# Parameter columns multiplied on TensorE at the start of six stages of a hybrid SSD and Hyena layer

## The chip, the cores and the metric

The kernel runs on one core of one Trainium2 chip. Its time is the device time of one execution in microseconds (us), as the median of several. The profile is a record of one execution, which the hardware profiler took. In what follows, PE is TensorE, PEld its weight loads, DVE VectorE, ACT ScalarE, POOL GpSimd, and SP the engine that issues most of the DMAs. A "record" is one entry of the trace: a 32-bit multiplication shows there as two matmuls with a weight load each.

## What is computed

One layer of a diffusion backbone with 2048 latent tokens of width 1024 and 256 context tokens. Two token mixers, a bidirectional Mamba-2 scan and an order-2 Hyena convolution, read the same normalized input through one projection; their outputs are gated, projected, merged and added to the input.

```python
h = rmsnorm(x, norm_w) * (1.0 + scale[:, None]) + shift[:, None]
...
cols = in_projection(h, w_in, ALL_IN_NAMES)
...
filt = hyena_filters(seqlen, w1, b1, w2, b2, w3, b3, freq, w_out)
h_bias = h_bias.astype(jnp.float32)
z = v
for o, gate in enumerate((x1, x2)):
    z = gate * (bidir_long_conv(z, filt[:, 0, o], filt[:, 1, o]) + h_bias[o] * z)
...
scores = jnp.einsum("bcqgn,bcsgn->bcqsg", cmat, bmat)
y_diag = jnp.einsum("bcqsg,bcqsgr,bcsgrp->bcqgrp", scores, decay, xdt)
y_off = jnp.einsum("bcqgn,bcgrpn,bcqgr->bcqgrp", cmat, start_states, jnp.exp(a_cs))
...
merged = (jax.nn.sigmoid(cols["g_m"]) * (ym @ w_branch_m)
          + jax.nn.sigmoid(cols["g_h"]) * (yh @ w_branch_h))
return merged @ w_out
```

## The kernel before

The kernel is a chain of stages, each a function with one instruction block per engine. A stage frees its semaphores at its end and all engines meet at a barrier (`Phase.release`, lines 68 and 67 in the trace); then the next stage's blocks begin. Nothing of a stage, not even a load, starts before that barrier, apart from a few loads of the first stages. Within a stage every engine's order is written out by hand, and semaphores tie the engines together. Data goes from one stage to the next through scratch tensors in HBM.

After the modulation, the normalization and the large input projection (until about 1630 us) come the six stages that matter here:

- **Taps** (`phase_taps_and_steps`, from 1636.6 us). PE multiplies the filters' hidden layer with the output weights (lines 1172 and 1174), eight matmuls of 512 columns into four banks, with the hidden layer split in a high part (line 1105, ACT) and a low part (line 1229, DVE). DVE multiplies each result with a decay window (line 1250) that ACT makes, and SP stores it as `kern_s`.
- **Spectra** (`phase_filter_spectra`, from 1785.8 us). The filters' Fourier transforms. SP loads `kern_s` in chunks into a ring of four buffers `spec_xin`; the load for chunk n waits until PE has used chunk n-4 (`s_a`). For each chunk PE runs `first` twice, each time four fp32 multiplications of 128x128 by 128 columns (line 1310), eight records. ACT and DVE copy the results out, and `second` (line 1323) multiplies them with a table. In the first block of 8 chunks there is only `first`; from the second block on, `first` of the block and `second` of the block before alternate.
- **Convolutions** (`phase_long_convs`, from 2029.4 us). Eight convolutions. PE's `first` (line 1527) is 64x64 matmuls on quarters of the array, `forward` is line 1567; DVE multiplies with the spectra (`product`, line 1696), for which SP loads six slots ahead, then the gate's inputs, then the next block's x, then further slots, in one queue.
- **States** (`phase_states`, from 2518.2 us). The scan's states, chunk by chunk: ACT and DVE weigh the inputs (lines 1833, 1858), PE multiplies (line 1807), DVE adds to the state (line 1877). The chunks' loads are all issued by SP, each into a buffer of its own.
- **Scan outputs** (`phase_ssd_outputs`, from 2634.6 us). PE makes scores (line 1978), then segment sums (line 1990) from masks that POOL and ACT spread (lines 1947, 2054), and the outputs from these.
- **Merge** (`phase_merge_output`, from 2917.0 us). 96 tiles of 24 matmuls each (lines 2304 to 2306: high and low parts of both operands). For the first tile DVE and ACT make high and low parts one `k` after another. After tile 0 PE forms two sums of squares (line 2314) from additions of POOL (line 2281), then goes on to tile 1.

In each of these stages PE's block begins with a wait for the stage's first loads or for what is made from them. `keep["par"]` is a small array of per-channel parameters, 128 partitions by 64 columns (`NPAR`) in fp32, that is loaded in the first stage and stays in SBUF.

Of the kernel before, what the change touches and what calls it, by code (L numbers as in the profile page):

```python
# [51 lines left out]

def banks(ph, n):
    return [ph.ps(f"bank{i}", [P, 512]) for i in range(n)]


class Phase:
# [951 lines left out]
def phase_taps_and_steps(nc, t, keep, tables, hid_s, kern_s, dt_c, dt_s, step_s):  # L1009
# [8 lines left out]
    with ExitStack() as ctx:  # L1018
# [106 lines left out]

        @block.tensor
        def _(pe):
            def reuse(k):
                if k >= 2:
                    name, i = slots[k - 2]  # L1130
                    if name == "taps":
                        pe.wait_ge(s_res, i + 1)
                    elif name == "turned":
                        pe.wait_ge(s_v, 2)
                    else:
                        pe.wait_ge(s_e, 3 * i + 3)
# [121 lines left out]
                    nc.vector.memset(res[:, o, SEQ:SEQ + 1], 0.0).then_inc(s_fix, 1)  # L1258


def phase_filter_spectra(nc, tables, kern_s, spec_s):

    NI = 2 * NBK
    GP = CB // 2
# [1 line left out]
    with ExitStack() as ctx:  # L1266
# [5 lines left out]
        bank = banks(ph, 8)  # L1272
# [25 lines left out]

        @block.tensor
        def _(pe):  # L1300
            def first(i, q):
                n = 16 * i + q
                if q % 2 == 0:
                    pe.wait_ge(s_ld[n // 2 % 4], loaded(n // 2))
                if n >= 4:
                    pe.wait_ge(s_ea, n - 3)
                    pe.wait_ge(s_ev, n - 3)
                for s in range(4):
                    g = 8 * (q % 2) + 2 * s
                    mm = pe.matmul(bank[n % 4][:, s * P:(s + 1) * P],  # L1310
                                   xin[:, n // 2 % 4, g:g + 2, :].rearrange("p g n -> p (g n)"), fk[:], start=True,
                                   stop=True)
                mm.then_inc(s_a, 1)
# [52 lines left out]
                    take(nc.vector.tensor_copy, i, q, 1, 1).then_inc(s_ev, 1)  # L1366


def phase_long_convs(nc, tables, u_s, z2_s, spec_s):

    NQ, NR, SLOT = 16, 8, 6
    NH, PS = NPL // 2, 4
    with ExitStack() as ctx:
# [134 lines left out]

        @block.tensor
        def _(pe):  # L1510
            def first(j, q):
                n, (blk, o) = NQ * j + q, convs[j]
                if o == 0 and q % 4 == 0:
# [216 lines left out]
def phase_states(nc, t, keep, tok_s, st_s, step_s, ssd):  # L1730
# [7 lines left out]
    with ExitStack() as ctx:  # L1738
# [49 lines left out]

        @block.tensor
        def _(pe):  # L1790
            def gates(s):
                for i in range(KT * KT * (s - G0) // GS, KT * KT * (s - G0 + 1) // GS):
                    m, k = i // KT, i % KT
                    if m % 4 == 0 and k == 0:
                        pe.wait_ge(s_aw[m // 4], 16)
                    mm = pe.matmul(gate[:, 2 * m:2 * m + 2], aw[:, m // 4, k, m % 4 * P:(m % 4 + 1) * P],
                                   keep["silu"][:, k, :], start=(k == 0), stop=(k == KT - 1))
                    if i == KT * KT - 1:
                        mm.then_inc(s_gate, 1)
# [85 lines left out]
            dve.wait_ge(s_gout, 1)  # L1885


def phase_ssd_outputs(nc, t, xbc_s, tok_s, st_s, z_s, g_s, ssd):

    with ExitStack() as ctx:  # L1890
        ph = Phase(nc, "y", ctx)
# [77 lines left out]

        @block.tensor  # L1970
        def _(pe):
            def scores(c):
                q = c % 2
                pe.wait_ge(s_bc[q], 16 * (c // 2) + 16)
# [177 lines left out]
def phase_merge_output(nc, t, keep, ym_s, z2_s, hg_s, gates_s, out):  # L2152
# [6 lines left out]
    with ExitStack() as ctx:  # L2159
# [132 lines left out]

        @block.tensor
        def _(pe):
            def tile(s, b, br, j):
                pe.wait_ge(s_wlo, s + 1)
                if s >= 4:
# [342 lines left out]
def program(nc, t, out):  # L2640
# [19 lines left out]
    with ExitStack() as ctx:  # L2660
# [18 lines left out]
        with ExitStack() as tctx:  # L2679
            tables = hyena_tables(Phase(nc, "tab", tctx))  # L2680
            phase_taps_and_steps(nc, t, keep, tables, hid_s, kern_s, dt_c, dt_s, step_s)
            phase_filter_spectra(nc, tables, kern_s, spec_s)
            phase_long_convs(nc, tables, u_s, z2_s, spec_s)
        with ExitStack() as sctx:
            ssd = ssd_buffers(Phase(nc, "ssd", sctx))
            phase_states(nc, t, keep, tok_s, st_s, step_s, ssd)
            phase_ssd_outputs(nc, t, xbc_s, tok_s, st_s, z_s, ym_s, ssd)
        phase_merge_output(nc, t, keep, ym_s, z2_s, hg_s, g_s, out)


# [28 lines left out]
```

## Time and profile before

| | us |
|---|---|
| Median of 3 executions | 3513.61 |
| Lowest and highest | 3512.41, 3515.05 |
| The profiled execution | 3513.2 |
| Its span, first to last instruction | 3511.1 |
| PE busy in it | 3228.8 (92%) |
| Mean granted clock of PE | 0.963 |

The granted clock is the share of full speed at which the throttle lets PE run; it has two levels here, 0.50 (1.2 GHz) and 1.00 (2.4 GHz). In a row of the timeline the bracket says how long the engine stood idle before the instruction and what released it. A wait for several semaphores is put down to the one that came last.

### The profile page before, as it was taken

To read this page: it belongs to the slowest core of one execution; us is meant where nothing else is said; L and a number is where in the kernel's file an instruction comes from. 1 tells how busy PE (TensorE), PEld (TensorE's weight loads), DVE (VectorE), ACT (ScalarE), POOL (GpSimd) and SP (SyncE) were. 2 spreads that over 40 slices of the span, in tenths; PEclk is the share of its full clock that TensorE was granted. 3 is DMA by queue.
4 is the path that set the end of the run, shared out by engine and by line. 5 is a ranking of instruction groups with operands and counts; after the bars stand their busy time and mean duration, and the time that the engine had idled before them with its cause. 6 is when DMAs were issued, how large, how long until landed. Compare 5 with 4: busy or idle time off the path is not lost. (4 is left out here: it accounts for less than half of the span.)

```text
span 3511.1 us, 55790 instructions
## 1 busy us (share of the span) xinstructions
PE 3228.8 (92%) x21878; PEld 2602.8 (74%) x21878; DVE 2080.1 (59%) x2495; ACT 1452.9 (41%) x2709; POOL 1948.4 (55%) x1324
## 2 busy tenths in 40 slices
PE   7899999999699999996679979999778997999998
PEld 3677888888588888885469956767566886788886
DVE  6697886223896884222754435555566775667662
ACT  4423222333433223333347745545447763333332
POOL 0486999777787998773100024343467763444542
PEclk9999999999799999998889989999989998999998
DMA  8444333332243323334899974664675665666562
GB/s 298 150 148 149 114 108 116 112 114 102 102 150 126 114 102 120 114 109 128 335 290 298 271 170 121 160 163 117 201 311 174 198 188 192 200 204 198 190 189 98
DMA packets 530472, 592.22 MB, mean 169 GB/s; under 512 B 287403, under 2 KB 408131, under 8 KB 527171
## 3 DMA queue, kind: packets, MB, share of 16 engines
q1 hardware_dynamic: 438957, 430.82, 40.7%
q10 hardware_dynamic: 91256, 157.83, 12.1%
q8 instruction: 176, 2.88, 0.4%
q14 instruction: 83, 0.68, 0.1%
HBM read 383.76 MB, written 204.80 MB: 168 GB/s over the span
## 5 line engine op out<-in xcount | busy, mean ns | idle before, releaser
L759 PE MATMUL pl_bank<-hl_hi,pl_a_hi 128*128 128x512 f32 x2056 | 813.6, 396 | 41.5 <-DVE hl_lo L391 27.8
L761 PE MATMUL pl_bank<-hl_hi,pl_a_lo 128*128 128x512 f32 x2056 | 804.9, 392 | 0.0
L760 PE MATMUL pl_bank<-hl_lo,pl_a_hi 128*128 128x512 f32 x2056 | 804.2, 391 | 0.0
L704 POOL TENSOR_TENSOR pl_a_lo<-hl_early_x,pl_a_hi 128x512 fp32r<-128x512 f32 x288 | 434.4, 1520 | 115.7 <-ACT pl_a_hi L808 115.6
L759 PEld LDWEIGHTS pl_bank<-hl_hi,pl_a_hi 128*128 128x128 f32 x2056 | 388.2, 189 | 129.3 <-DVE hl_lo L391 28.0
L761 PEld LDWEIGHTS pl_bank<-hl_hi,pl_a_lo 128*128 128x128 f32 x2056 | 388.4, 189 | 82.5
L760 PEld LDWEIGHTS pl_bank<-hl_lo,pl_a_hi 128*128 128x128 f32 x2056 | 389.0, 189 | 78.0
L808 ACT ACTIVATE pl_a_hi<-hl_early_x 128x512 fp32r<-128x512 f32 x288 | 181.8, 633 | 540.3 <-PE pl_bank L761 444.6
L2276 POOL TENSOR_TENSOR mo_w_lo<-mo_w,mo_w_hi 128x1024 fp32r<-128x1024 f32 x96 | 238.1, 2482 | 277.1 <-ACT mo_w_hi L2347 277.1
L704 POOL TENSOR_TENSOR pl_a_lo<-hl_w,pl_a_hi 128x512 fp32r<-128x512 f32 x220 | 312.3, 1433 | 114.6 <-ACT pl_a_hi L808 114.5
L2304 PE MATMUL mo_bank<-mo_hi,mo_w_hi 128*128 128x512 f32 x768 | 305.8, 398 | 20.6 <-POOL mo_w_lo L2276 17.2
L958 DVE SCALAR_TENSOR_TENSOR pl_res<-hl_early_w,pl_taps,pl_res 128x1023 f32<-128x1023 f32 (+1 forms) x160 | 312.3, 1952 | 3.0
L2306 PE MATMUL mo_bank<-mo_hi,mo_w_lo 128*128 128x512 f32 x768 | 300.7, 392 | 0.0
L2305 PE MATMUL mo_bank<-mo_lo,mo_w_hi 128*128 128x512 f32 x768 | 300.5, 391 | 0.0
L1506 POOL TENSOR_TENSOR conv_both<-conv_prod 128x256 f32<-128x256 f32 x128 | 93.6, 732 | 282.8 <-DVE conv_prod L1691 207.2
L808 ACT ACTIVATE pl_a_hi<-hl_w 128x512 fp32r<-128x512 f32 x220 | 138.0, 629 | 258.8 <-PE pl_bank L761 252.0
L699 POOL TENSOR_TENSOR hl_early_x<-hl_w 128x512 f32<-128x512 f32 x144 | 214.7, 1491 | 12.2 <-POOL pl_a_lo L704 12.2
L1696 DVE TENSOR_TENSOR conv_prod<-conv_front,conv_spec 128x1024 f32<-128x1024 f32 x120 | 141.9, 1219 | 90.5 <-PE conv_front L1567 67.2
L2304 PEld LDWEIGHTS mo_bank<-mo_hi,mo_w_hi 128*128 128x128 f32 x768 | 144.8, 189 | 56.6 <-issue 18.2
L1665 ACT COPY conv_v<-conv_inv 128x512 f32<-128x512 f32 x128 | 126.2, 1066 | 141.3 <-PE conv_inv L1583 141.3
L1336 DVE COPY spec_y<-spec_bank 64x256 f32<-64x256 f32 x256 | 109.5, 428 | 124.0 <-PE spec_bank L1310 121.9
L2305 PEld LDWEIGHTS mo_bank<-mo_lo,mo_w_hi 128*128 128x128 f32 x768 | 145.1, 189 | 30.9 <-issue 1.9
(237 smaller groups left out, 6026.4 us busy)
## 6 DMA issues: line engine op xcount, KB each, us to landing
hl_w<-in_w_rec SPq DMA_DIRECT2D x146, 512.0 KB, 3.6
mo_w<-in_w_br SPq DMA_DIRECT2D x96, 512.0 KB, 3.7
kern_s<-taps_res SPq DMA_DIRECT2D x16, 2048.0 KB, 7.0
spec_s<-spec_res ACTq DMA_DIRECT2D x128, 256.0 KB, 3.7
conv_spec<-spec_s SPq DMA_DIRECT2D x240, 128.0 KB, 2.9
g_s<-pl_res ACTq DMA_DIRECT2D x32, 512.0 KB, 2.6
spec_xin<-kern_s SPq DMA_DIRECT2D x32, 512.0 KB, 5.9
spec_xin<-kern_s SPq DMA_DIRECT2D x128, 128.0 KB, 3.8
```

Source lines behind the costliest of these rows:

```text
L699: nc.gpsimd.tensor_tensor(sums[:, i], x, y, op).then_inc(s_sum, 1)
L704: nc.gpsimd.tensor_tensor(a_lo[:, at % NS, :], src, a_hi[:, at % NS, :].bitcast(F32), ALU.subtract).then_inc(s_lo, 1)
L759: pe.matmul(out, a_hi[:, q, m], op_hi[:, b, k, :], start=begin, stop=False)
L760: pe.matmul(out, a_hi[:, q, m], op_lo[:, b, k, :], start=False, stop=False)
L761: return pe.matmul(out, a_lo[:, q, m], op_hi[:, b, k, :], start=False, stop=end)
L808: nc.scalar.activation(a_hi[:, n % NS, :], src, ACT.Copy).then_inc(s_hi, 1)
L958: nc.vector.scalar_tensor_tensor(out=dst, in0=src[:, i:i + width], scalar=taps[i], in1=dst, op0=ALU.mult, op1=ALU.add).then_inc(s_conv, 1)
L1696: nc.vector.tensor_tensor(prod[:, n % PS], u[:, None].to_broadcast([P, 2, 2, CB]), spec[:, m % SLOT, :, None].to_broadcast([P, 2, 2, CB]), ...
L2276: nc.gpsimd.tensor_tensor(w_lo[:, s % 3, :], w[:, s % 3, :], w_hi[:, s % 3, :].bitcast(F32), ALU.subtract).then_inc(s_wlo, 1)
L2304: pe.matmul(bank[s % 4][:], w_hi[:, q, m], hi[:, slot, k, :], start=(k == 0), stop=False)
L2305: pe.matmul(bank[s % 4][:], w_hi[:, q, m], lo[:, slot, k, :], start=False, stop=False)
L2306: mm = pe.matmul(bank[s % 4][:], w_lo[:, q, m], hi[:, slot, k, :], start=False, stop=(k == KT - 1))
```

## The change

A helper issues n times the same multiplication: 128 partitions, 64 stationary columns and 64 moving columns, both of them `keep["par"]`, into a 64x64 corner of a PSUM bank. Nothing reads the corner; the stage's real work overwrites it or leaves it alone. The multiplications wait for nothing and signal nothing. PE's block of six stages begins with such a call, ahead of everything else; `keep` is passed to the three functions that did not have it. The counts are 80 (taps), 75 (spectra), 30 (convolutions), 48 (states), 30 (scan outputs) and 82 (merge).

```diff
+def keep_busy(pe, out, src, n):
+
+    for _ in range(n):
+        pe.matmul(out, src, src, start=True, stop=True)
...
+            keep_busy(pe, ps[1][0:NPAR, 0, 0:NPAR], keep["par"][:, 0:NPAR], 80)
...
-def phase_filter_spectra(nc, tables, kern_s, spec_s):
+def phase_filter_spectra(nc, keep, tables, kern_s, spec_s):
...
         @block.tensor
         def _(pe):
+            keep_busy(pe, bank[7][0:NPAR, 0:NPAR], keep["par"][:, 0:NPAR], 75)
+
             def first(i, q):
...
+            keep_busy(pe, front[1][0:NPAR, 1, 0:NPAR], keep["par"][:, 0:NPAR], 30)
...
+            keep_busy(pe, gate[0:NPAR, 64:64 + NPAR], keep["par"][:, 0:NPAR], 48)
...
+            keep_busy(pe, p_seg[0][0:NPAR, 0:NPAR], keep["par"][:, 0:NPAR], 30)
...
+            keep_busy(pe, bank[3][0:NPAR, 0:NPAR], keep["par"][:, 0:NPAR], 82)
```

Line numbers in the changed kernel are 6 to 18 higher. In PE's order, the start of the spectra stage before, where the two branches are the stage's boundary, `spec_bank` the stage's eight banks and `spec_xin` the loaded chunks:

```order
L1174 MATMUL taps_ps<-taps_hid_lo,taps_ws 128x512
L1018 UNCONDITIONAL_BRANCH
L1299 UNCONDITIONAL_BRANCH
L1310 MATMUL spec_bank<-tab_fk,spec_xin 128x128 x68
L1323 MATMUL spec_bank<-spec_y,tab_wf 128x256 x2
L1310 MATMUL spec_bank<-tab_fk,spec_xin 128x128 x4
```

And in the changed kernel:

```order
L1182 MATMUL taps_ps<-taps_hid_lo,taps_ws 128x512
L1024 UNCONDITIONAL_BRANCH
L1307 UNCONDITIONAL_BRANCH
L60 MATMUL spec_bank<-keep_par 64x64 x75
L1320 MATMUL spec_bank<-tab_fk,spec_xin 128x128 x68
L1333 MATMUL spec_bank<-spec_y,tab_wf 128x256 x2
```

The 75 stand ahead of the first chunk's matmuls, and nothing else has moved. PE's start of the scan output stage before, where `y_p_sc` are the scores and `y_p_seg` the segment sums:

```order
L1738 UNCONDITIONAL_BRANCH
L1970 UNCONDITIONAL_BRANCH
L1978 MATMUL y_p_sc<-y_bc 128x128 x4
L1990 MATMUL y_p_seg<-y_spread,ssd_after 128x512 x16
L1978 MATMUL y_p_sc<-y_bc 128x128 x4
```

And in the changed kernel:

```order
L1750 UNCONDITIONAL_BRANCH
L1984 UNCONDITIONAL_BRANCH
L60 MATMUL y_p_seg<-keep_par 64x64 x30
L1994 MATMUL y_p_sc<-y_bc 128x128 x4
L2006 MATMUL y_p_seg<-y_spread,ssd_after 128x512 x16
L1994 MATMUL y_p_sc<-y_bc 128x128 x4
```

The 30 stand ahead of the first scores; between these and the segment sums nothing was put.

## Rows read from the trace of the kernel before

**Rows 1.** The page: the whole execution's span.
```profile
span 3511.1 us, 55790 instructions
```
**Rows 2.** Stretches: length, busy by PE, PEld, DVE, ACT, POOL, granted clock, DMA share, GB/s.
```profile
1785.80:1790.06 4.26, 0.00 (x1) 0.00 (x1) 0.00 (x0) 0.00 (x0) 0.00 (x0) 0.50 0.83 172
1790.06:1793.80 3.74, 3.74 (x17) 3.74 (x18) 0.85 (x2) 0.80 (x2) 0.00 (x0) 0.50 1.37 223
1793.80:1797.40 3.60, 3.60 (x33) 3.45 (x31) 3.35 (x8) 3.23 (x8) 0.00 (x0) 1.00 1.38 217
2033.60:2046.40 12.80, 10.42 (x355) 10.09 (x356) 4.42 (x10) 4.42 (x10) 0.00 (x0) 0.50 0.89 175
2644.20:2647.10 2.90, 2.89 (x7) 2.33 (x8) 0.12 (x1) 0.81 (x3) 2.90 (x2) 0.50 1.02 407
2928.00:2933.80 5.80, 5.58 (x12) 3.56 (x12) 5.47 (x7) 2.84 (x4) 2.42 (x1) 0.50 1.05 392
```
**Rows 3.** Timeline, spectra stage, SP and PE: start, us, engine, instruction, [idle <-releaser].
```profile
1785.79 0.37 SPq L1291 DMA_DIRECT2D spec_xin<-kern_s  x1
1790.06 3.57 PE L1310 MATMUL spec_bank<-tab_fk,spec_xin 128*128 128x128 f32 x15 [21.32 <-DMA spec_xin<-kern_s]
1793.87 0.77 SPq L1291 DMA_DIRECT2D spec_xin<-kern_s  x1
...
1799.84 2.05 PE L1310 MATMUL spec_bank<-tab_fk,spec_xin 128*128 128x128 f32 x16 [0.36 <-DMA spec_xin<-kern_s]
...
1809.47 1.16 PE L1310 MATMUL spec_bank<-tab_fk,spec_xin 128*128 128x128 f32 x8 [0.36 <-DMA spec_xin<-kern_s]
```
**Rows 4.** PE's instruction groups, 1812 to 2009 us: busy, mean ns, idle.
```profile
L1310 PE MATMUL spec_bank<-tab_fk,spec_xin 128*128 128x128 f32 x884 | 116.6, 275 | 0.0
```
**Rows 5.** Weight loads of 128 and 64 columns, ns min/median/max.
```profile
L1310 PEld LDWEIGHTS spec_bank<-tab_fk,spec_xin x1024: 186/192/333, 1790.1 to 2006.6; 128*128 128x128 f32 x171
L1567 PEld LDWEIGHTS conv_front<-conv_y,tab_wf x1024: 132/137/230, 2052.0 to 2487.8; 128*64 128x64 f32 x171
```
**Rows 6.** Timeline, taps stage: PE's second set, VectorE's first products.
```profile
1659.86 0.80 PE L1172 MATMUL taps_ps<-taps_hid_hi,taps_ws 128*128 128x512 f32 x1 [6.37 <-DVE taps_hid_lo L1229]
1662.18 4.49 DVE L1250 TENSOR_TENSOR taps_res<-taps_ps,taps_window 128x2048 f32<-128x2048 f32 x2 [2.38 <-ACT taps_window L1110]
```
**Rows 7.** Timeline, convolution stage: SP's loads, VectorE's wait.
```profile
2065.90 4.30 SPq L1446 DMA_DIRECT2D conv_spec<-spec_s  x4
2072.75 3.49 DVE L1696 TENSOR_TENSOR conv_prod<-conv_front,conv_spec 128x1024 f32<-128x1024 f32 x3 [8.60 <-DMA conv_spec<-spec_s]
```
**Rows 8.** Timeline, state stage: SP's first load, VectorE.
```profile
2518.15 0.33 SPq L1769 DMA_DIRECT2D ssd_tail<-step_s  x1
2529.91 1.22 DVE L1877 TENSOR_TENSOR st_state<-st_faded,st_s 128x1024 f32<-128x1024 f32 x1 [0.51 <-PE st_s L1807]
2533.11 0.82 DVE L1858 TENSOR_TENSOR st_wx<-st_xb,st_tail 128x640 f32<-128x640 f32 x1 [1.98 <-DMA st_xb<-tok_s]
```
**Rows 9.** Timeline, scan output stage, PE's first matmuls.
```profile
2638.93 2.08 PE L1978 MATMUL y_p_sc<-y_bc 128*128 128x128 f32 x8 [5.93 <-DMA y_bc<-xbc_s]
2644.21 3.43 PE L1990 MATMUL y_p_seg<-y_spread,ssd_after 128*128 128x512 f32 x8 [3.20 <-ACT y_spread L2054]
```
**Rows 10.** Timeline, merge stage: SP's first load, PE, POOL's additions.
```profile
2916.95 0.36 SPq L2215 DMA_DIRECT2D mo_yT<-z_s  x1
2928.04 0.76 PE L2304 MATMUL mo_bank<-mo_hi,mo_w_hi 128*128 128x512 f32 x1 [16.07 <-POOL mo_w_lo L2276]
...
2938.88 5.01 POOL L2281 TENSOR_TENSOR mo_ms<-mo_ms,mo_odd 128x512 f32<-128x512 f32 x4 [4.74 <-ACT mo_odd L2367]
2940.48 2.10 PE L2314 MATMUL mo_ssq<-mo_ms,mo_ones 128*128 128x512 f32 x4
2942.02 0.80 PE L2304 MATMUL mo_bank<-mo_hi,mo_w_hi 128*128 128x512 f32 x1
```
**Rows 11.** Waits, 2915 to 2990 us: total us, times, longest.
```profile
PEld mo_ssq L2314 <- POOL mo_ms L2281: 0.9, 2, 0.7
```

More of the change, by code:

```diff
@@ L1366, in _, with phase_long_convs @@
                     take(nc.vector.tensor_copy, i, q, 1, 1).then_inc(s_ev, 1)
-def phase_long_convs(nc, tables, u_s, z2_s, spec_s):
+def phase_long_convs(nc, keep, tables, u_s, z2_s, spec_s):
     NQ, NR, SLOT = 16, 8, 6
@@ L1885, in _, with phase_ssd_outputs @@
             dve.wait_ge(s_gout, 1)
-def phase_ssd_outputs(nc, t, xbc_s, tok_s, st_s, z_s, g_s, ssd):
+def phase_ssd_outputs(nc, t, keep, xbc_s, tok_s, st_s, z_s, g_s, ssd):
     with ExitStack() as ctx:
@@ L2681, in program @@
             phase_taps_and_steps(nc, t, keep, tables, hid_s, kern_s, dt_c, dt_s, step_s)
-            phase_filter_spectra(nc, tables, kern_s, spec_s)
-            phase_long_convs(nc, tables, u_s, z2_s, spec_s)
+            phase_filter_spectra(nc, keep, tables, kern_s, spec_s)
+            phase_long_convs(nc, keep, tables, u_s, z2_s, spec_s)
         with ExitStack() as sctx:
@@ L2686, in program @@
             phase_states(nc, t, keep, tok_s, st_s, step_s, ssd)
-            phase_ssd_outputs(nc, t, xbc_s, tok_s, st_s, z_s, ym_s, ssd)
+            phase_ssd_outputs(nc, t, keep, xbc_s, tok_s, st_s, z_s, ym_s, ssd)
         phase_merge_output(nc, t, keep, ym_s, z2_s, hg_s, g_s, out)
```

## The prediction

> **What bounds the kernel now.** I start from the span, 3511.1 us [rows 1], and ask of each of the six stages what releases it at its start and what it runs at after that. I read the granted clock in short stretches first, since the change can only work through it. PE does start on the lower level of its clock (0.50, 1.2 GHz): in the spectra stage it does nothing from SP's first load at 1785.79 to its first matmul at 1790.06, and its clock stands at 0.50 until 1793.8, then at 1.00 (2.4 GHz) [rows 2, 3]. The scan output stage (2644.2 to 2647.1) and the merge stage (2928.0 to 2933.8) show the same [rows 2]. So the clock rises 2.9 to 5.8 us after PE begins to work, 3.7 in the spectra stage. The second question is whether those cold matmuls are late for anybody. That is read from the timelines, from who waits last.
>
> In the spectra stage it is the loads: PE's chunks of 16 records begin at 1799.84 and on to 1809.47, each after some 0.36 us of waiting for spec_xin [rows 3], with the DMA share at 1.37 to 1.38 [rows 2]. Five chunk starts lie in 9.63 us, 2.4 us each. After that PE sets the pace: from 1812 to 2009 us it has no idle time before the 884 records of line 1310 [rows 4]. What the stage loses before 1810 is therefore lost at its end.
>
> **What a parameter matmul costs.** It isn't in the trace. A 64x64 fp32 multiplication of 128 rows should be two records, as line 1310's are (884 in the stretch where the code has half as many), each with a weight load. The nearest row is line 1310, with 128 columns: 17 records in 3.74 us, 0.220 us each, at 0.50, and 33 in 3.60 us, 0.109 us each, at 1.00 [rows 2]. Half the columns halves both the stream and the load of the weights (median 192 ns for 128 columns against 137 for 64: 55 ns for 64 columns) [rows 5]. I take 0.110 us cold and 0.055 warm per record. The upper bound is the whole price of line 1310. The lower one is line 1527, the small 64x64 matmuls of the convolution stage: 355 records in 10.42 us, 0.029 us each, at 0.50 [rows 2]. Line 1527 works on quarters of the array, several at a time, while the new ones all use the same half, so I stay with the half price.
>
> **Spectra stage, 75 of them, 150 records.** PE can start them when the stage begins, about 1785.8, with the clock at 0.50. If it rises after 4.4 us (the middle of 2.9 and 5.8), 40 records are done by then, and 110 more take 6.0 us: PE is free at 1796.3. With 2.9 and 5.8 us it is 1795.5 and 1797.0. The first chunk has been there since 1790.06, so PE comes 5 to 7 us late. It is then warm, but that isn't enough, since the ring of four buffers stops the loads: SP's fifth load waits until PE has used up the first chunk. Now it is issued at 1793.87, about 0.3 us after 1790.06 + 16 x 0.22 = 1793.6, and its data starts the chunk at 1799.84 [rows 3]. Afterwards the first chunk ends at 1796.3 + 16 x 0.109 = 1798.0 and the load is issued at 1798.3. By then the queue has run dry (the fourth chunk's data is in at about 1797.4, one pace of 2.4 us before 1799.84), and a load into an idle queue takes 1790.06 - 1785.79 = 4.27 us [rows 3]: 1802.6. That is 2.7 us behind 1799.84 (2.0 to 3.4 with the other two rises). From there the loads go at their old pace of 2.4 us and PE, with 1.75 us of work in each, can't make them come sooner. The warm start itself is worth nothing here. **+2.7 us**, kept to the end of the stage.
>
> **Taps stage, 80.** Nothing. They lie in PE's wait for its first weights; after its first eight matmuls PE waits another 6.37 us for VectorE's low halves, starting again at 1659.86, and VectorE's first products at 1662.18 are released by ScalarE's window [rows 6]. PE's eight next matmuls end before the second product.
>
> **Convolution stage, 30.** PE's first 512 records get shorter, by at most half of the 10.42 us at 0.50 [rows 2], 5.2 us. But VectorE then stands 8.60 us, until 2072.75, for a spectrum load that SP issues at 2065.90 behind its other loads, in an order and at a pace that PE has no hand in [rows 7]. Anything from 5.2 us early to 8 us late vanishes in it. Zero.
>
> **State stage, 48.** 96 records are 4.4 + 56 x 0.055 = 7.5 us from 2518.15: 2525.7. Sixteen records of 256 columns at twice 0.109 end at 2529.2, no later than VectorE's second state at 2529.91. It next waits for a load until 2533.11 anyway [rows 8]. Zero.
>
> **Scan output stage, 30.** Some 3.3 to 6.6 us (60 records at either price), against PE's 5.93 us of idle time before 2638.93; the scores from there on get 1 us shorter. Then PE waits for ScalarE's spreads until 2644.21 [rows 9]. It is at 0.50 there now [rows 2]. If it stayed at 1.00, the first segment's four matmuls would be ready some 0.85 us sooner (half of the 3.43 us for eight, for half of them), and everything behind them. But the wait before them stays, 3.20 us and more, as the scores end sooner, and an idle PE loses the clock: in the taps stage PE, idle for 6.37 us after its first eight matmuls, takes 0.80 us for the next one [rows 6], as long as the merge stage's first (0.76 us) at 0.50 [rows 10]. I take zero and keep 0.85 as the other end. The Trainium skill (TensorE: Matmul & The Clock Gate, "HAM oscillation — how this bites in real kernels") says the same against this insertion: a burst shorter than the wait behind it has to begin cold again; by that rule the sum is +2.7 us, and without it +1.9.
>
> **Merge stage, 82.** 164 records from 2916.95 take 4.4 + 124 x 0.055 = 11.2 us: 2928.2, on time for 2928.04 [rows 10]. The first tile is at 0.50 for 5.58 us [rows 2], so up to 2.8 us could be won. It is fed by VectorE, one pair of halves at a time. Behind it PE needs POOL's additions: the first of four begins at 2938.88, each takes 5.01 / 4 = 1.25 us, so the second is ready at 2941.4. PE does wait for them (0.9 us in 2 waits), and the next tile follows at 2942.02 [rows 10, 11]. An earlier end of the first tile meets that wait. Zero.
>
> The sum is +2.7 us. The profiled execution took 3513.2 us with its 3511.1 us span, 0.4 us under the median 3513.61, so I add to the median: **3516.3 us**.
>
> **Rivals.** (a) The insertions are cheap and hidden everywhere. At 0.029 us a record the 75 take 4.4 us, the length of the spectra stage's wait, and nothing moves: 3513.6. Line 1527's price speaks for it, the halves of rows 5 against it. Beside the rows: the Trainium skill (TensorE: Matmul & The Clock Gate, "Back-to-back issue gap") gives some 60 cycles, about 25 ns, for up to 64 columns; by that price too the change would be free. (b) Slower: the clock doesn't rise on these narrow matmuls. In the convolution stage it stayed at 0.50 through 12.8 us of 64-column work, PE busy for 10.42 of them [rows 2]. Then the spectra stage's 150 records end at 1802.3, the first chunk takes 3.5 us cold, and the fifth load lands at 1802.3 + 3.5 + 0.3 + 4.27 = 1810.4: +10.5 us. In the merge stage 164 x 0.110 is 18.0 us, PE starts at 2935.0, and the tile's 24 matmuls, twelve in 5.6 us as now and twelve in half of that, end at 2943.4; with 1.5 us for the sums (2940.48 to 2942.02) that is 2.9 us late: 3527.0. The full price of line 1310 would give about as much. It decides from 0.083 us per warm record, twice that cold: 4.4 us cold and 10.3 warm for the 150, PE free at 1800.5, and a loss of 7.0 us in the spectra stage alone. Against it: there is no gap in these matmuls, and in all stages the clock rose within 5.8 us of dense work. (c) Faster: the cold stretches are on the path after all. Half of 3.74, 10.42, 2.89 and 5.58 us is 11.3 us; with the 2.7 lost, 3505.0. It needs VectorE and POOL to wait for PE where the rows show loads and additions.
>
> **How the numbers follow.** The forecast, 3516.3, gets 0.62: its own range is 3515.5 to 3517.2. (a) gets 0.15, (b) 0.15, (c) 0.05; 0.03 is for other shifts, such as PE's instruction fetches falling elsewhere. A measurement of this kernel can tell about 0.2%, 7.0 us. Forecast and (a) lie within it. (b) lies above, but a mild form of it doesn't. (c) is just beyond. So faster 0.05, same 0.80, slower 0.15. The range goes from 3511.5, which takes in (a) with the 1.2 us by which the runs of before fall under their median, to 3521.0, where the spectra stage costs 7.4 us by a dearer record.
>
> **What would show it.** In the timeline the 150 records run from 1785.8 to 1796.3, PE's first real matmul there starts at about 1796, five to seven us later than its data, and SP's fifth load is issued at about 1798. The stage's end, and every later stage, lies 2.7 us later. PE's clock is at 1.00 when it starts on spectra and on the merge tile. VectorE's wait of 8.6 us in the convolution stage stays, about as long; the scan's first segments are still at 0.50; the second merge tile starts as long after the stage's begin as before, 25.1 us. I would be wrong if PE's first real matmul there stayed at its load's landing (a), if the clock were 0.50 until after it (b), or if the stretch from the stage's start to the second tile shrank (c).

## The result, and the profile of the changed kernel

| | before | changed |
|---|---|---|
| Median of 20 executions each, us | 3513.05 | 3519.61 |
| Lowest and highest, us | 3509.3, 3518.46 | 3515.37, 3524.35 |
| Span of the profiled execution, us | 3511.1 | 3517.4 |
| Mean granted clock of PE | 0.963 | 0.971 |

The ratio is 1.0017 with a 95% interval of 1.0011 to 1.0023. On 3513 us that is 6.0 us more, 3.9 to 8.1. The clock did rise, and the kernel got slower. The time lies within the predicted range and within the 0.2% called no change, but 3.3 us above the forecast of 3516.3 and outside the forecast's own range, and where 2.7 us were forecast to be lost, 6.0 were.

The page's first line and its line on the queue of TensorE's instruction fetches (packets, MB, share). The queue had 176 packets in the kernel before:

```profile
span 3517.4 us, 57170 instructions
...
q8 instruction: 181, 2.97, 0.4%
```

Stretches of the changed kernel, with the columns of [rows 2]:

```profile
1781.50:1786.50 5.00, 4.98 (x47) 5.00 (x48) 0.00 (x0) 0.00 (x0) 0.00 (x0) 0.50 0.91 183
1786.50:1792.60 6.10, 6.10 (x106) 6.08 (x104) 0.00 (x0) 0.00 (x0) 0.00 (x0) 1.00 1.20 195
1792.60:1796.30 3.70, 3.70 (x35) 3.65 (x33) 2.35 (x6) 2.24 (x6) 0.00 (x0) 1.00 0.11 26
2641.50:2644.40 2.90, 0.81 (x2) 0.74 (x3) 1.17 (x2) 1.94 (x7) 2.90 (x1) 0.50 1.12 361
2932.10:2937.90 5.80, 3.82 (x12) 1.94 (x12) 5.64 (x7) 2.73 (x4) 2.41 (x1) 1.00 1.05 396
```

A parameter record costs 4.98 / 47 = 0.106 us at 0.50 and 6.10 / 106 = 0.058 us at 1.00. PE now begins the spectra and the merge stage at 1.00, where [rows 2] had 0.50. The third row is the important one: while PE is at full clock on its first real chunks, the DMA share is down to 0.11, where it was 1.38 for the first chunks at full clock before. The scan output stage's first segments are still at 0.50.

The start of the spectra stage, PE's timeline and one load of SP (the fifth of the stage), to be held against [rows 3]:

```profile
1781.52 11.20 PE L60 MATMUL spec_bank<-keep_par 128*64 128x64 f32 x150 [15.17 <-PEq L74]
1792.65 10.98 PE L1320 MATMUL spec_bank<-tab_fk,spec_xin 128*128 128x128 f32 x96
1803.95 2.05 PE L1320 MATMUL spec_bank<-tab_fk,spec_xin 128*128 128x128 f32 x16 [0.31 <-DMA spec_xin<-kern_s]
1806.39 2.05 PE L1320 MATMUL spec_bank<-tab_fk,spec_xin 128*128 128x128 f32 x16 [0.40 <-DMA spec_xin<-kern_s]
1809.64 1.16 PE L1320 MATMUL spec_bank<-tab_fk,spec_xin 128*128 128x128 f32 x8 [1.19 <-DMA spec_xin<-kern_s]
```

```profile
1794.73 0.36 SPq L1299 DMA_DIRECT2D spec_xin<-kern_s  x1
```

SP's first load is at 1781.48, so PE's first real matmul comes 11.2 us into the stage, and the fifth load is issued 13.25 us into it. Before, these were 4.3 and 8.1 us [rows 3]. Six chunks (96 records) then run without a wait. From the seventh on, PE waits for loads again. The ninth chunk, with which the stage's PE-bound part begins, starts at 1809.64, 28.2 us after the stage's first load; before it was 1809.47 - 1785.79 = 23.7. So 4.5 of the 5.0 us by which the stage is longer (248.6 against 243.6) are there by the ninth chunk. PE's matmuls of `first` from 1815 to 2009 us have no idle time before them, as in [rows 4]:

```profile
L1320 PE MATMUL spec_bank<-tab_fk,spec_xin 128*128 128x128 f32 x872 | 114.9, 275 | 0.0
```

The rows that answer to [rows 6, 7, 9], from the timelines of the taps, convolution and scan output stage:

```profile
1659.69 0.80 PE L1180 MATMUL taps_ps<-taps_hid_hi,taps_ws 128*128 128x512 f32 x1 [6.33 <-DVE taps_hid_lo L1237]
...
2073.07 3.48 DVE L1708 TENSOR_TENSOR conv_prod<-conv_front,conv_spec 128x1024 f32<-128x1024 f32 x3 [5.68 <-DMA conv_spec<-spec_s]
...
2643.59 3.51 PE L2006 MATMUL y_p_seg<-y_spread,ssd_after 128*128 128x512 f32 x8 [2.25 <-ACT y_spread L2070]
```

And the merge stage's first tile, for [rows 10, 11]: two rows of PE's timeline and one of the waits.

```profile
2939.28 0.50 PE L2322 MATMUL mo_bank<-mo_hi,mo_w_hi 128*128 128x512 f32 x1 [2.40 <-DVE mo_lo L2445]
...
2940.48 0.79 PE L2322 MATMUL mo_bank<-mo_hi,mo_w_hi 128*128 128x512 f32 x1 [0.24 <-DVE mo_lo L2445]
```

```profile
PEld mo_ssq L2332 <- POOL mo_ms L2297: 1.2, 2, 0.9
```

The faster matmuls wait for VectorE's low halves, and at 2940.48 a matmul takes 0.79 us again: the clock was given back within the first tile. At its end PE waits for POOL's additions, as before.

Below, the length of each stage is taken from SP's first load of the stage to that of the next one (the merge stage to the span's end). "Ninth chunk" is the start of the 129th record of the spectra stage's `first`, counted from the stage's first load. All in us, one traced execution each; the labels are those of the experiments. The merge column can be 0.1 us low.

| kernel | taps | spectra | ninth chunk | conv. | states | scan out | merge |
|---|---|---|---|---|---|---|---|
| before | 149.2 | 243.6 | 23.7 | 488.7 | 116.4 | 282.4 | 594.0 |
| e7, before once more | 148.1 | 243.6 | 23.7 | 488.6 | 115.7 | 284.0 | 595.6 |
| changed | 145.3 | 248.6 | 28.2 | 487.2 | 116.7 | 285.6 | 597.8 |
| e1, spectra's 75 alone | 147.9 | 246.4 | 26.6 | 490.6 | 115.2 | 284.0 | 598.5 |
| e2, all but spectra's | 146.5 | 244.4 | 24.5 | 485.8 | 117.4 | 282.3 | 597.6 |
| e3, spectra's, 150 | 148.5 | 255.9 | 35.9 | 488.5 | 116.2 | 285.8 | 597.8 |
| e4, changed, ring of 8 | 147.0 | 246.2 | 25.1 | 489.3 | 116.4 | 284.2 | 597.9 |
| e5, before, ring of 8 | 147.9 | 243.9 | 23.7 | 488.3 | 115.9 | 284.2 | 595.6 |
| e6, conv.'s, 90 | 147.1 | 243.8 | 23.7 | 490.1 | 115.2 | 284.0 | 597.9 |
| e8, taps', 64 | 147.9 | 243.8 | 23.7 | 488.1 | 116.0 | 284.3 | 595.9 |
| e9, taps', 90 | 147.2 | 244.7 | 24.6 | 487.5 | 115.7 | 284.3 | 598.1 |
| e10, changed, taps' 55 | 145.9 | 247.1 | 27.2 | 490.0 | 115.9 | 283.9 | 595.1 |
| e11, 30 behind the scores | 148.0 | 243.5 | 23.7 | 488.4 | 116.1 | 284.1 | 595.4 |
| e12, the same once more | 147.5 | 243.7 | 23.7 | 489.8 | 117.0 | 282.7 | 595.7 |

Two lengths move with the kernel and not with the execution: spectra, which was predicted, and merge, which was not. The other four vary by 2 to 5 us with no such pattern. In e2 and e9 the ninth chunk is 0.8 and 0.9 us late although nothing was put into their spectra stage; that is taken up further below.

### The profile page after: what moved, and what is told of

Same layout as the page of the kernel before. It is cut to its first block and busy times, and to the rows that moved or that the text cites. A ratio compares the mean times of both kernels' runs of the same rounds, so it can differ in the third digit from the quotient of the medians.

```text
span 3517.4 us, 57170 instructions
## 1 busy us (share of the span) xinstructions
PE 3271.3 (93%) x22568; PEld 2644.2 (75%) x22568; DVE 2074.3 (59%) x2495; ACT 1451.8 (41%) x2709; POOL 1947.0 (55%) x1324
## 5 line engine op out<-in xcount | busy, mean ns | idle before, releaser
L705 POOL TENSOR_TENSOR hl_early_x<-hl_w 128x512 f32<-128x512 f32 x144 | 216.0, 1500 | 12.2 <-POOL pl_a_lo L710 12.2
```

The lines of the kernel that those rows point to most:

```text
L705: nc.gpsimd.tensor_tensor(sums[:, i], x, y, op).then_inc(s_sum, 1)
```

## Experiments on the spectra stage

The theory was the prediction's: PE late by a few us, carried to the stage's end by the ring of four buffers. Rivals: the loss is made elsewhere, or the insertions cost by themselves.

**e1 and e2: which stage loses.** e1 keeps only the 75 of the spectra stage:

```diff
-            keep_busy(pe, ps[1][0:NPAR, 0, 0:NPAR], keep["par"][:, 0:NPAR], 80)
...
-            keep_busy(pe, front[1][0:NPAR, 1, 0:NPAR], keep["par"][:, 0:NPAR], 30)
...
-            keep_busy(pe, gate[0:NPAR, 64:64 + NPAR], keep["par"][:, 0:NPAR], 48)
...
-            keep_busy(pe, p_seg[0][0:NPAR, 0:NPAR], keep["par"][:, 0:NPAR], 30)
...
-            keep_busy(pe, bank[3][0:NPAR, 0:NPAR], keep["par"][:, 0:NPAR], 82)
```

and e2 removes only these 75:

```diff
-            keep_busy(pe, bank[7][0:NPAR, 0:NPAR], keep["par"][:, 0:NPAR], 75)
```

> Only the 75 multiplications of the spectra stage are kept. My theory: nearly the whole loss comes from there, because PE comes late to the first chunk and the ring of four buffers passes the delay to the loads. In the trace of the changed kernel the eighth chunk's successor starts 28.2 us after the stage's first load against 23.7 before, and the stage is 5.0 us longer. So this kernel should be 3.5 to 5.5 us slower than before, with PE's first real matmul 11.2 us after SP's first load. Rival: the loss is spread, since in the traces the scan output stage is 3.1 us longer and the merge stage 3.7 us longer too; then this kernel is only 1 to 3 us slower than before.

Measured: 3519.27 against 3513.24, ratio 1.0016 (1.0008 to 1.0025), 5.6 us.

> The five other insertions are kept (80, 30, 48, 30, 82) and the 75 of the spectra stage left out. My theory: within 1 us of before, either way, as each of the five is hidden by a wait that PE has no part in. Rival (spread loss): 3 us or more slower, with the scan output and merge stages longer by about 3 us each, as in the one trace of the changed kernel. Second rival (the gain was real but covered by the spectra stage's loss): 2 us or more faster.

Measured: 3515.35, ratio 1.0003 (0.9995 to 1.0012). So the kernel with the spectra stage's insertion alone is slower beyond its noise, and the one with the five others isn't; but the two intervals overlap, and by the medians e2 is 2.1 us slower too. That the other five are free is not shown by these times. And e1's trace leaves something over: its ninth chunk is 2.9 us late, as forecast, and its merge stage is 598.5 us, though nothing was put there.

**e3: is every further us lost?** The 75 of e1 doubled.

```diff
-            keep_busy(pe, bank[7][0:NPAR, 0:NPAR], keep["par"][:, 0:NPAR], 75)
+            keep_busy(pe, bank[7][0:NPAR, 0:NPAR], keep["par"][:, 0:NPAR], 150)
```

> Only the spectra stage's insertion, doubled from 75 to 150. Each further multiplication is two records of 0.056 us at full clock, 0.112 us, so 75 more are 8.4 us. My theory: once PE is later than the loads need, each microsecond of it is a microsecond of the kernel, so this kernel is 8.4 us slower than the one with 75, 12 to 14 us slower than before. Rival: part of a delay is caught up behind the loads later in the stage; then the second 75 cost clearly less or more than 8.4 us.

Measured: 3527.01, ratio 1.0035 (1.0023 to 1.0048). The ninth chunk comes 35.9 us into the stage, 12.2 us late. PE's timeline of e3:

```profile
1785.25 19.03 PE L60 MATMUL spec_bank<-keep_par 128*64 128x64 f32 x300 [16.76 <-PEq L74]
1804.20 10.98 PE L1319 MATMUL spec_bank<-tab_fk,spec_xin 128*128 128x128 f32 x96
1816.33 2.05 PE L1319 MATMUL spec_bank<-tab_fk,spec_xin 128*128 128x128 f32 x16 [1.14 <-DMA spec_xin<-kern_s]
```

PE's first real matmul is 8.6 us later than in e1 (19.0 against 10.4 us after the first load), the ninth chunk 9.3 us and the stage's end 9.5 us. By the medians the kernel is 7.7 us slower than e1, where 8.4 were expected. About a us is lost for a us of delay, as a chain of loads that waits for PE would give it.

**e4 and e5: is it the ring?** e4 is the changed kernel, e5 the kernel before, both with eight buffers for `spec_xin`:

```diff
-        xin = ph.sb("xin", [P, 4, 16, NA])
+        xin = ph.sb("xin", [P, 8, 16, NA])
...
-                    if n >= 4:
-                        sp.wait_ge(s_a, 2 * (n - 4) + 2)
+                    if n >= 8:
+                        sp.wait_ge(s_a, 2 * (n - 8) + 2)
```

> The changed kernel with eight buffers for spec_xin instead of four. Theory (the ring carries the loss): the fifth to eighth loads no longer wait for TensorE, so TensorE, starting about 11.2 us after the stage's entry, reaches the ninth chunk after 8 x 1.75 us, at 25.2 us, where the loads alone would allow 23.7. The spectra stage takes 245 to 245.5 us (before 243.6, changed kernel 248.6) and the kernel is about 1.7 us slower than before, a ratio of 1.0005 and 3 to 4 us less than the changed kernel. Rival (the loss comes from the late start or from the insertions themselves, whatever the ring): the stage stays at 248 to 249 us and the ratio at 1.0015 or more.

> The kernel before with eight buffers for spec_xin and no insertion: the control of the run with eight buffers. Theory: at the stage's start the loads themselves set the pace, 2.4 us a chunk, so the deeper ring gives at most 1 us: stage 243 to 244 us, ratio 0.9997 to 1.0003. Rival: loads of this stage waited for TensorE already, and the deeper ring alone is worth 3 us or more (stage under 241 us); then the run with eight buffers and insertions says less about the insertions.

PE's timeline of e4:

```profile
1782.17 10.75 PE L60 MATMUL spec_bank<-keep_par 128*64 128x64 f32 x150 [15.22 <-PEq L74]
1792.85 15.45 PE L1320 MATMUL spec_bank<-tab_fk,spec_xin 128*128 128x128 f32 x136
```

All nine first chunks (136 records) now run without one wait. The ninth starts at 25.1 us, as expected, 1.4 us late instead of 2.9 to 4.5: the ring is what carries the rest. The stage, 246.2 us, is somewhat longer than the 245 to 245.5 expected. In e5 the ninth chunk starts at 23.7 us, so the deeper ring alone gives nothing. PE's timeline of e5, whose first load is at 1783.57:

```profile
1807.25 1.16 PE L1318 MATMUL spec_bank<-tab_fk,spec_xin 128*128 128x128 f32 x8 [0.34 <-DMA spec_xin<-kern_s]
```

As times: e5 3513.70, ratio 1.0001 (0.9992 to 1.0010), as expected. e4 3518.51, ratio 1.0017 (1.0008 to 1.0026), and that was a miss: 1.0005 was expected. The ring did what it should and the kernel stayed slow, by 5.3 us by the medians, of which the spectra stage holds 2.3. The rest had to be elsewhere.

**e6: a late start where another wait covers it.** Only the convolution stage's insertion, 90 instead of 30.

```diff
-            keep_busy(pe, front[1][0:NPAR, 1, 0:NPAR], keep["par"][:, 0:NPAR], 30)
+            keep_busy(pe, front[1][0:NPAR, 1, 0:NPAR], keep["par"][:, 0:NPAR], 90)
```

> Only the convolution stage's insertion, with 90 multiplications instead of 30: TensorE's first real matmul there comes about 12.8 us after the stage's entry instead of 4.3. Theory: with the warm clock some 3 to 5 us of that are left when TensorE hands over, and VectorE's wait of 8.6 us for its spectrum load takes it up: the wait gets shorter by that, the stage stays at 486 to 490 us, ratio 1.0000. Rival (a late start of TensorE is paid in any stage): the stage and the kernel are 4 to 8 us longer.

Measured: 3516.87, ratio 1.0006 (0.9997 to 1.0015). The convolution stage took 490.1 us; in the nine traces with no insertion there it took 487.5 to 490.6. VectorE's timeline of e6 where [rows 7] had its wait of 8.60 us:

```profile
2063.45 2.35 DVE L1706 TENSOR_TENSOR conv_prod<-conv_front,conv_spec 128x1024 f32<-128x1024 f32 x2 [0.48 <-PE conv_front L1577]
2067.39 2.36 DVE L1706 TENSOR_TENSOR conv_prod<-conv_front,conv_spec 128x1024 f32<-128x1024 f32 x2 [1.59 <-PE conv_front L1577]
2071.20 2.36 DVE L1706 TENSOR_TENSOR conv_prod<-conv_front,conv_spec 128x1024 f32<-128x1024 f32 x2 [1.45 <-PE conv_front L1577]
```

VectorE's first product there comes 32.8 us after the stage's first load, against 22.7 and 23.7 in the two traces of before. The load wait has gone altogether, and the ninth product, which had waited for that load, comes at 45.1 us against 43.3 and 43.6. So 1.5 to 1.8 of the 9 to 10 us are left, which the stage's length can't show. The 3.6 us by which the kernel is slower by the medians are not clear of noise, and the trace has a longer merge stage beside them (597.9 us). A late start of PE costs only what no later wait takes up. The expected 3 to 5 us of lateness was too little; that it would be absorbed was right.

## Experiments on the merge stage

**e7: is 594 us against 598 only the execution?** The kernel before once more.

> The kernel before once more, for a second trace of it. The lengths of its stages should repeat within about 1 us where TensorE sets the pace; the merge stage was 594.0 us in the first trace and 597.6 to 598.5 us in four traces of changed kernels, two of them without an insertion there. If it is again near 594, something in the changed kernels lengthens the merge stage by 4 us; if it is near 598, that is the variation of one execution.

Merge stage 595.6 us, as in e5, the other kernel without insertions. So the six traces with insertions by then (597.6 to 598.5) differ from the three without (594.0 to 595.6). Broken down by tile, most of it is in two places, before tile 1 and at tiles 10 and 11. A third, 0.5 to 0.8 us at tile 40, is in most traces with insertions and also in e5, which has none, so it isn't the insertions'. "To tile 1" is from the stage's first load to PE's first matmul of tile 1; "fetch" is when an instruction fetch of PE starts in the stage near its loads for tiles 10 and 11. In us:

| kernel | to tile 1 | tile 10 | tile 11 | fetch |
|---|---|---|---|---|
| before | 25.1 | 6.69 | 5.60 | 87.7 |
| e7 | 25.8 | 6.66 | 5.59 | 88.0 |
| e5 | 25.5 | 6.83 | 5.61 | 88.0 |
| e1 | 25.3 | 8.01 | 7.17 | 79.3 |
| e2 | 26.2 | 7.61 | 5.59 | 78.9 |
| e3 | 25.1 | 8.34 | 7.16 | 74.7 |
| e4 | 26.7 | 7.33 | 5.57 | 73.9 |
| e6 | 25.1 | 7.70 | 7.22 | 72.2 |
| changed | 26.4 | 8.38 | 5.61 | 75.2 |

PE's instructions come in packets of 16 KB, of which 181 instead of 176 were counted above. The changed kernel has 690 more of PE's records, and 690 / 5 is 138; between two fetches of the merge stage some 125 lie. So one packet holds about 128 records, that is 64 of these multiplications. If so, whatever is inserted before moves all later fetches, unless it is a multiple of 64. The loads for tiles 10 and 11 are issued in one burst, 71 to 81 us into the stage, and in all six of these kernels with insertions, whatever stage they were in, a fetch falls into it. The Trainium skill (Runtime: NRT & Kernel Launch, "Instruction fetch mechanics") gives the same size, 16 KiB blocks of 256 instructions, and says that crossing into a new block is mostly hidden. The first part agrees: 64 multiplications of two weight loads and two matmuls each are 256 instructions. The second is what was tested, and in this burst a fetch is not hidden.

**e8, e9, e10: a whole packet or not.** e8 and e9 have only the taps stage's insertion, with 64 and with 90; e10 is the changed kernel with 55 there, 320 in all, which is five packets.

```diff
-            keep_busy(pe, ps[1][0:NPAR, 0, 0:NPAR], keep["par"][:, 0:NPAR], 80)
+            keep_busy(pe, ps[1][0:NPAR, 0, 0:NPAR], keep["par"][:, 0:NPAR], 64)
```

> Only the taps stage's insertion, with 64 multiplications, and nothing in the other five stages. In every kernel with insertions the merge stage took 597.6 to 598.5 us, in three traces without any 594.0 to 595.6, and there TensorE's instruction fetches (one 16 KB packet for about 128 of its matmul records) fall 52.5 and 88 us into the merge stage, with insertions at 72 to 79 us, in the middle of the burst of loads for tiles 10 and 11. Theory (the place of the fetches): 64 multiplications are 128 records and so one whole fetch, which leaves the later fetches where they were: fetches at 52 to 53 and 88 us again, merge stage 594 to 596 us, no fetch in the burst; spectra stage 243.6 to 244; ratio 0.9997 to 1.0003. Rival (any insertion, or more code, lengthens the merge stage): 597.5 us or more and a ratio of 1.0005 to 1.0010.

> Only the taps stage's insertion, with 90 multiplications: 26 more than one whole fetch, the same rest as in the kernel with 90 in the convolution stage. Theory (the place of the fetches): they fall about 72 us into the merge stage, in the burst of loads; that stage takes 597.5 to 598.5 us; ratio about 1.0007. Rival (the place doesn't matter): as with 64 in the same stage, within 0.5 us in the merge stage.

> The changed kernel with 55 instead of 80 multiplications in the taps stage: 320 in all, five whole fetches, where the changed kernel has 25 more than five. Theory (two causes that add): the fetches in the merge stage are back at 52 to 53 and 88 us and that stage is 2 to 3 us shorter than in the changed kernel, 594.5 to 596 us, while the spectra stage keeps its loss (247 to 248.6 us against 243.6). In all 3 to 4 us slower than before, ratio 1.0010. Rival (no second cause): merge stage 597.5 us or more and the changed kernel's ratio, 1.0017.

The DMA queues from 71 to 81 us into the merge stage (packets, MB, share), e8:

```profile
q1 hardware_dynamic: 1475, 3.28, 90.9%
q14 instruction: 1, 0.01, 0.2%
```

and e9:

```profile
q1 hardware_dynamic: 1458, 3.24, 90.1%
q8 instruction: 1, 0.02, 0.6%
q14 instruction: 1, 0.01, 0.2%
```

e9 has the fetch (q8) and e8 doesn't. What follows in e8 (first load of the stage at 2916.50), one row each of SP, ACT and PE:

```profile
2990.60 0.44 SPq L2219 DMA_DIRECT2D mo_w<-in_w_br  x1
...
2997.00 1.06 ACT L2355 ACTIVATE mo_w_hi<-mo_w 128x1024 fp32r<-128x1024 f32 x1 [5.16 <-DMA mo_w<-in_w_br]
...
3000.56 0.50 PE L2312 MATMUL mo_bank<-mo_hi,mo_w_hi 128*128 128x512 f32 x1 [1.32 <-POOL mo_w_lo L2284]
```

and in e9 (first load at 2916.21):

```profile
2990.31 1.19 SPq L2219 DMA_DIRECT2D mo_w<-in_w_br  x1
...
2997.89 1.06 ACT L2355 ACTIVATE mo_w_hi<-mo_w 128x1024 fp32r<-128x1024 f32 x1 [4.66 <-DMA mo_w<-in_w_br]
...
3001.44 0.50 PE L2312 MATMUL mo_bank<-mo_hi,mo_w_hi 128*128 128x512 f32 x1 [2.50 <-POOL mo_w_lo L2284]
```

With the fetch, which starts 74.0 us into the stage, SP's issue at 74.1 us takes 1.19 us instead of 0.44. ACT's row is released by the weights of an earlier issue, at 72.8 us (72.7 in e8): they land 1.2 us later after the stage's start (81.7 against 80.5), and PE's wait for tile 11's low halves, behind ACT and POOL, is 2.50 us instead of 1.32. So the held issue isn't what makes them late. The burst's first load, issued at 70.7 us in e9 and 70.8 in e8, lands late too, at 76.4 against 74.7 us: all that is under way lands later. In e9 there is a second loss on top. The stretch of tile 11, e8:

```profile
3000.60:3006.10 5.50, 5.50 (x24) 4.57 (x25) 2.15 (x2) 2.10 (x3) 5.50 (x3) 1.00 0.58 156
```

and e9:

```profile
3001.40:3008.50 7.10, 7.06 (x24) 5.67 (x25) 2.24 (x2) 2.10 (x3) 6.84 (x3) 0.76 0.53 168
```

After the longer wait the clock fell to 0.50 for a part of the tile, which makes it 1.6 us longer (7.17 against 5.58 from tile to tile). Together with tile 10's 1.2 us (8.10 against 6.92) that is 2.8 us, less 0.6 gained at tiles 16 and 40: the 2.2 us by which the stages differ, 598.1 against 595.9. The spectra stage adds 0.9 us, 244.7 against 243.8.

As times, of kernels that ran side by side: e8 3511.95, ratio 1.0000 (0.9991 to 1.0008), e9 3516.39, ratio 1.0009 (1.0000 to 1.0018). That is twenty-six multiplications more, in a wait that hides them, and 4.4 us by the medians, 3.1 by the means. The two intervals overlap a good deal, so the times agree with the traces' 3.1 us (2.2 and 0.9) but wouldn't show it alone. e10: 3516.99, ratio 1.0014 (1.0005 to 1.0023), merge stage 595.1, with tile 10 at 6.80 and tile 11 at 5.59, and its ninth chunk still 3.5 us late. Its time is between e8's and the changed kernel's, as two causes that add would have it, but its interval overlaps with both of theirs; it is the trace that separates them.

**e11 and e12: full clock for the first segments.** The last prediction step to test was that a burst ahead of the scores can't warm the segments behind a wait. Here the 30 stand in that wait, and nowhere else:

```diff
+            keep_busy(pe, p_seg[0][0:NPAR, 0:NPAR], keep["par"][:, 0:NPAR], 30)
```

> 30 multiplications in the scan output stage alone, put behind the first scores, in TensorE's wait of 3.2 us for the first segments, and none elsewhere. Theory: with no idle time in front of them the first segments begin at the full clock: the first four of their matmuls, 0.43 us each at 0.50, take half, and the first segment is ready about 0.85 us sooner; the stage of 282.4 to 284.2 us gets at most 1 us shorter, which one time can't show. Rival: the clock stays at 0.50 all the same, or the 30 end after the spread's landing (6 us at the lower clock against a wait of 3.2) and the segments start up to 2 us late.

PE's timeline of e11 (first load of the stage at 2631.34):

```profile
2637.88 4.49 PE L60 MATMUL y_p_seg<-keep_par 128*64 128x64 f32 x60
2642.29 2.12 PE L2001 MATMUL y_p_seg<-y_spread,ssd_after 128*128 128x512 f32 x8
2645.57 1.20 PE L2001 MATMUL y_p_seg<-y_spread,ssd_after 128*128 128x512 f32 x4 [1.15 <-DVE y_weight L2112]
```

and of e7, without them (first load at 2632.08):

```profile
2641.70 3.75 PE L1990 MATMUL y_p_seg<-y_spread,ssd_after 128*128 128x512 f32 x8 [3.60 <-ACT y_spread L2054]
2645.82 1.86 PE L1990 MATMUL y_p_seg<-y_spread,ssd_after 128*128 128x512 f32 x4 [0.36 <-DVE y_weight L2100]
```

The eight matmuls take 2.12 us instead of 3.75, and start 1.3 us later (10.95 against 9.62 us), because the 60 records ran over the spread's landing. The next segments start 14.2 us into the stage against 13.7. Nothing is gained: both halves of the expectation came true and cancel.

Its trace was also the exception in the other matter: 30 multiplications, a fetch at 72.5 us, and yet a merge stage of 595.4 us. So the same kernel was timed:

> The kernel with 30 multiplications behind the first scores once more, now timed. Its first trace is the exception to the theory of the fetches' place: a fetch 72.5 us into the merge stage, in the burst of loads, and yet a merge stage of 595.4 us. Theory 1 (a fetch in the burst costs 2 to 3 us, in most executions): this trace shows 597.5 to 598.5 us and the timed ratio is 1.0005 to 1.0010, less the 0.85 us that the warm segments may give. Theory 2 (it is not enough that the fetch falls into the burst, and this kernel escapes every time): 595 to 596 us again and a ratio of 0.9995 to 1.0003.

Measured: 3513.36 against 3514.13, ratio 1.0002 (0.9993 to 1.0011); merge stage 595.7, tile 10 7.32, tile 11 5.57, fetch at 72.2 us. That is theory 2: in both of its traces the kernel escapes. The fetch costs it 0.6 us at tile 10, and the clock stays up. e6 has its fetch at the same 72.2 us and loses both, 7.70 and 7.22. Its packet took 1.99 us where e12's took 1.09, and PE's wait before tile 11 was 2.10 us against 1.72, which no run isolates. That a fetch falls into the burst is therefore necessary for the loss in these traces, but how much it costs depends on more than its time, and that stays open.

## Where the prediction was right and where it wasn't

**The price and the clock: right.** 0.110 and 0.055 us per record were taken, 0.106 and 0.058 measured. The clock rose 5.0 us after the insertion's start (3.3 in e1), within 2.9 to 5.8. Rival (a), with its 0.029 us, and rival (b), in which the clock stays low, fell with these two numbers.

**The ring in the spectra stage: right, and undersized.** PE was to be free 10.5 us into the stage and the load chain to be 2.7 us late. PE was free at 10.4 in e1, where the ninth chunk is 2.9 us late, but at 11.2 in the changed kernel, where the later rise of the clock and the dearer warm record cost 0.7 us. That makes 3.4. One detail of the working was wrong without harm: the fifth chunk, which was to start at 1802.6, doesn't wait for its load, since PE, itself late, only gets to it 18.4 us after the stage's first load. The prediction's own numbers had this in them: four chunks of 1.75 us from 1796.3 are 1803.3. The wait shows from the seventh chunk on. The ninth is 4.5 us late, so some 1 us is still missing, and it has a row: SP's tenth load, in whose issue, 3.71 us long, a fetch of PE falls.

```profile
1803.66 3.71 SPq L1299 DMA_DIRECT2D spec_xin<-kern_s  x1
```

The queues from 1803 to 1807 us show that fetch beside the loads:

```profile
q1 hardware_dynamic: 3390, 0.86, 133.8%
q8 instruction: 1, 0.02, 2.0%
```

That it delays the ninth chunk is seen in the kernels that have nothing in this stage. In e9 a fetch starts 17.8 us after the stage's first load, in e2 20.0 us, and their ninth chunks come at 24.6 and 24.5 us. In the seven others the nearest fetch starts between 22.5 and 27.4 us, and the ninth chunk comes at 23.7. In e9's timeline of PE the eighth chunk has the wait, with some 1 us more than the usual 0.36:

```profile
1806.11 2.05 PE L1318 MATMUL spec_bank<-tab_fk,spec_xin 128*128 128x128 f32 x16 [1.38 <-DMA spec_xin<-kern_s]
```

e10, which differs from the changed kernel by 25 multiplications in the taps stage, says the same: its fetch starts at 26.0 us instead of 24.1, PE's first real matmul is at 11.0 us as against 11.2, and the ninth chunk comes at 27.2 us instead of 28.2. So some 0.8 to 0.9 us of the loss in the spectra stage is a fetch's too.

**The five zeros: right for four of them as far as the traces show, not for the merge stage.** The taps stage's wait for VectorE stayed, 6.33 us after 6.37. In the convolution stage VectorE's load wait took up what came, 5.68 us after 8.60; e3, with nothing inserted there, has 5.63, so the shorter wait need not be the insertion's. The first segments were at 0.50 again, 3.51 us after 3.43, but not as the prediction had it. PE's timeline of the changed kernel:

```profile
2634.01 3.68 PE L60 MATMUL y_p_seg<-keep_par 128*64 128x64 f32 x60 [1.64 <-PEq L74]
2639.53 1.81 PE L1994 MATMUL y_p_sc<-y_bc 128*128 128x128 f32 x8 [1.84 <-DMA y_bc<-xbc_s]
```

The 60 records ran at 1.00 from the start, and the clock fell at 2639.85, among the scores. In e4 and e10 the eight scores too ran at 1.00 (1.16 us), and after waits of 2.38 and 4.13 us the eight segments took 3.75 us, at 0.50. The rule that was taken there from the Trainium skill (TensorE: Matmul & The Clock Gate, "HAM oscillation — how this bites in real kernels") came true in its result, a cold start behind the wait. Its condition as it was put there, a burst shorter than the wait, was not met in this trace: the records took 3.68 us, and the waits behind them were 1.84 and 2.25 us.

In the merge stage the warm first matmuls ended in waits for VectorE and POOL. Tile 1 starts 26.4 us after the stage's first load, and 26.0 to 26.7 in all four kernels with an insertion there, against 25.1 to 25.8 in the ten traces without. This is about 1 us later, not zero. In the changed kernel SP's fourth load took 2.49 us to issue where both traces of before have 0.43, with a fetch beside it; in each of the four a fetch starts within the stage's first 9 us, and in none of the ten. So whether the 82 multiplications or the fetch costs this was not separated. e2, with these five and without the spectra stage, has a ratio of 1.0003 (0.9995 to 1.0012), which leaves room for up to 4 us. Rival (c), gains from the cold stretches, has nothing to show.

**The step that failed: "other shifts, such as PE's instruction fetches falling elsewhere", at 0.03 and no size.** It was the second cause. The 345 multiplications are 25 more than five packets, and that puts a fetch into the merge stage's load burst, where tile 10 then takes 8.38 us instead of 6.7. The merge stage is 2.2 to 3.8 us longer than in the two traces of before, 2.7 longer than in e10, which differs by 25 multiplications in the taps stage. Of these 2.7 us, 1.6 are tile 10's and 0.4 lie before tile 1; 0.8 are at tile 40, as in e5 and e8, whose bursts have no fetch, so these are not the burst's. Against the second trace of before, the spectra stage is 5.0 us longer, the merge stage 2.2, and the others some 1.5 us shorter together, which is the difference of the spans, 3517.4 - 3511.7 = 5.7 us; 6.0 (3.9 to 8.1) was measured. That the time still lay in the predicted range is in part luck: its upper end, 3521.0, had been set for a dearer record, and no fetch was in it. The taps stage took 145.3 to 147.9 us in the kernels with insertions there and 147.1 to 149.2 in those without; whether that is an effect was not looked into.

No version beat the kernel before. By their times e5, e8 and e12 equal it.

## What to carry to other kernels

Multiplications that keep the clock up have a chance only where PE's next real work is what everyone waits for, and where they end before it could start; here no stage met both, so that they pay there was not shown. Past that point, in front of a ring of loads that PE has to free, each us of overrun is about a us at the end of the stage (e3), unless a later wait is long enough to swallow it (e6). And any edit that adds instructions to PE moves all later instruction fetches: before a small difference in a far stage is explained, compare where the fetches fall, and repeat the edit padded to a whole packet.

## What the runs showed of the hardware that was not expected

- PE's instructions arrive in packets of 16 KB, one for about 128 of its matmul records. A single one that falls into a burst of loads at 90% of the queues' time held an issue of SP for 1.19 us instead of 0.44, and loads that were already under way landed 1.2 to 1.7 us later (e9 against e8). In front of the four-buffer ring of the spectra stage one made the ninth chunk 0.8 to 0.9 us late (e2, e9). The transfer itself takes about 1 us (0.94 us in e9). How it holds up 3 MB of loads was not shown.
- Before tile 11, a wait of PE of 2.50 us (e9) was followed by half the clock for a part of the tile, and cost 1.6 us on top; so were waits of 2.10 us (e6), 2.40 us (e1) and 2.73 us (e3). Waits of 1.32 us (e8), 1.68 us (e11) and 2.01 us (e2) were not, but neither was one of 2.78 us in the changed kernel, so the wait's length alone doesn't decide:

```profile
3006.30 0.50 PE L2322 MATMUL mo_bank<-mo_hi,mo_w_hi 128*128 128x512 f32 x1 [2.78 <-POOL mo_w_lo L2292]
```

- In the convolution stage VectorE's first product came 9 to 10 us later and its ninth only 1.5 to 1.8 us later (e6): a wait for a load had taken up the rest.
